# The last up group of quarter 0 as seven products of half blocks, in both feed-forwards

## The reference

```
    h = _rms_norm(x, norm_ffn_pre[i])                                      # first block
    f = jnp.square(jax.nn.relu(h @ w_ffn_up[i])) @ w_ffn_down[i]
    x = x + _rms_norm(f, norm_ffn_post[i])
...
    h = rms_norm(x, norm_mlp[l])                                           # second block
    x = x + jnp.square(jax.nn.relu(h @ w_up[l])) @ w_down[l]
```

## Time and profile before

| what | value |
|---|---|
| median of 3 runs | 1240.69 us (1240.66 to 1241.28) |
| profiled execution, its own time | 1239.91 us |
| its span | 1238.2 us, mean granted TensorE clock 0.997 |
| PE busy | 1205.6 us (97%) |
| DVE busy | 871.9 us (70%) |
| ACT busy | 664.1 us (54%) |
| POOL busy | 420.7 us (34%) |

### The profile page before, as it was taken

One profiled execution on the slowest core, in us unless ns is written; L12 is line 12 of the kernel. 1 busy time (PEld: TensorE's weight loads), 2 busy tenths in 40 slices (PEclk: granted clock), 3 DMA queues, 4 the chain that ended last, 5 costly groups with the idle time before them and its releaser, 6 DMA issues.

```text
span 1238.2 us, 26863 instructions
## 1 busy us (share of the span) xinstructions
PE 1205.6 (97%) x11189; PEld 1103.8 (89%) x11189; DVE 871.9 (70%) x1153; ACT 664.1 (54%) x1154; POOL 420.7 (34%) x345
## 2 busy tenths in 40 slices
PE   8999999998999999999999999999999999999998
PEld 6777797787898999999999997866889999999997
DVE  6678646566468689887895666435576897888953
ACT  4555536557355447456475544544454474564652
POOL 7022226333005247267261141000052472672500
PEclk9999999999999999999999999999999999999999
DMA  6223300002343233333344232122232333333331
GB/s 203 69 68 102 102 2 2 4 3 81 131 150 121 69 103 104 102 103 113 92 171 154 77 107 82 35 69 86 69 101 70 103 103 103 103 107 99 103 120 69
DMA packets 103231, 113.10 MB, mean 91 GB/s; under 512 B 2099, under 2 KB 97381, under 8 KB 103110
## 3 DMA queue, kind: packets, MB, share of 16 engines
q1 hardware_dynamic: 103030, 111.12, 28.4%
q0 software_dynamic: 80, 0.26, 0.1%
HBM read 107.18 MB, written 4.19 MB: 90 GB/s over the span
## 4 chain that ended last, share of the span: by engine, by line
PE 84%; DVE 7%; ACT 4%; issue 2%; DVEq 1%; ACTq 1%; POOL 1%; POOLq 0%
PE ps L627 8%; PE ps L628 7%; PE ps L629 7%; PE ps L718 5%; PE ps L719 5%; PE ps L720 5%; PE ps L591 4%; PE ps L593 4%; PE ps L592 4%; PE ps L773 3%; PE ps L775 3%; PE ps L774 3%; PE ps L678 1%; PE ps L680 1%; PE ps L679 1%
## 5 line engine op out<-in xcount | busy, mean ns | idle before, releaser
L627 PE MATMUL ps<-w_hi,a_hi 128*128 128x256 f32 x640 | 179.5, 280 | 0.3
L628 PE MATMUL ps<-w_lo,a_hi 128*128 128x256 f32 x640 | 178.8, 279 | 0.0
L629 PE MATMUL ps<-w_hi,a_lo 128*128 128x256 f32 x640 | 178.5, 279 | 0.0
L2065 DVE TENSOR_TENSOR w_lo<-w_raw,w_hi 128x2048 fp32r<-128x2048 f32 (+1 forms) x43 | 98.1, 2282 | 45.5 <-ACT w_hi L1398 45.2
L627 PEld LDWEIGHTS ps<-w_hi,a_hi 128*128 128x128 f32 x640 | 120.2, 188 | 1.2 <-DVE w_lo L2194 1.1
L628 PEld LDWEIGHTS ps<-w_lo,a_hi 128*128 128x128 f32 x640 | 120.3, 188 | 0.1
L629 PEld LDWEIGHTS ps<-w_hi,a_lo 128*128 128x128 f32 x640 | 120.3, 188 | 0.0
L718 PE MATMUL ps<-th,w_hi 128*128 128x256 f32 x384 | 109.2, 284 | 1.6 <-ACT tmp L1496 1.6
L720 PE MATMUL ps<-th,w_lo 128*128 128x256 f32 x384 | 107.9, 281 | 0.0
L719 PE MATMUL ps<-tl,w_hi 128*128 128x256 f32 x384 | 107.8, 281 | 0.0
L2173 DVE TENSOR_TENSOR w_lo<-w_raw,w_hi 128x1024 fp32r<-128x1024 f32 (+1 forms) x72 | 100.0, 1403 | 4.4 <-ACT w_hi L1471 4.4
(11 more groups left out here) (467 smaller groups left out, 3885.2 us busy)
## 6 DMA issues: line engine op xcount, KB each, us to landing
w_raw<-w_ffn_up_dram SPq DMA_DIRECT2D x16, 1024.0 KB, 5.7
w_raw<-w_ffn_down_dram SPq DMA_DIRECT2D x16, 1024.0 KB, 5.3
w_raw<-w_up_dram SPq DMA_DIRECT2D x16, 1024.0 KB, 5.8
w_raw<-w_down_dram SPq DMA_DIRECT2D x16, 1024.0 KB, 5.2
w_raw<-w_in_first_dram SPq DMA_DIRECT2D x12, 1024.0 KB, 5.4
w_raw<-w_out_dram SPq DMA_DIRECT2D x8, 1024.0 KB, 5.2
xn<-x_dram SPq DMA_DIRECT2D x8, 512.0 KB, 6.0
w_raw<-w_in_dram SPq DMA_DIRECT2D x4, 1024.0 KB, 6.3
```

The lines of the kernel that those rows point to most:

```text
L627: mm(o, hi[:, hb + k, tok], whi, start=first and own and k == ks[0], stop=False, skip_group_check=True)
L628: mm(o, hi[:, hb + k, tok], wlo, start=False, stop=False, skip_group_check=True)
L629: m = mm(o, lo[:, hb + k, tok], whi, start=False, stop=last and k == ks[-1], skip_group_check=True)
L2065: v.tensor_tensor(w_lo[:, g % 2, :, 0:n], w_raw[:, g % 2, :, 0:n], w_hi[:, g % 2, :, 0:n].bitcast(F32), ALU.subtract).then_inc(sm["w_lo_re ...
```

## The change

In both feed-forwards group 3 of quarter 0 becomes seven products. `seven(0)` is now `range(3, 4)`. Its blocks need room in both slots of `w_hi` and `w_lo`: `A11` and `A12` take the place of channels 0 to 511 of group 2, `SUM2` and `SUM1` that of channels 512 to 1023 of group 2, and `SUM3`, `SUM4` and `A22` lie in the slot that groups 1 and 3 share. So group 2 is now run in halves of the channels (`third_group`): both tiles with channels 0 to 511, a signal (`third_half`), then both tiles with channels 512 to 1023. It has the same 48 matmuls of 512 columns.

POOL makes the four sums of group 3 directly after its activation sums, ahead of the sums of squares. ACT does the four `upper_t` in one go and then the six upper parts of group 3, and only then the square of the second tile of group 1; the two tiles of group 2 are evacuated while group 3 runs. DVE does all four `lower_t` and then six lower parts in the order `A11, SUM3, SUM4, A22, SUM2, SUM1`. The rest of the order is that of a last up group of the other quarters: the first plain down group is split in two halves (`down_upper`, `down_lower`), and results are copied and added in pieces. On SP the load of the second down group now also waits for the sums and the lower part of `A22` of group 3.

```diff
         def seven(q):
-            return range(4 if q else 0)
+            return range(4) if q else range(3, 4)
...
         def block_free(b, q, u, n):
             g = group(b, q, u)
+            if q == 0:
+                return done(g - 1 if n in (SUM3, SUM4, A22) else g)
...
# SP
+                        if q == 0 and c == 1:
+                            sp.wait_ge(sm["wb_lo"], block_at(b, 0, 3, A22))
+                        if c + 2 in seven(q) and c < 2:
                             sp.wait_ge(sm["s_sum"], 4 * seventh(b, q, c + 2) + 4)
...
# TensorE
+            def third_group(b):
+                g, tile = group(b, 0, 2), tile_at(b, 0, 2)
+                for half in range(2):
+                    if half:
+                        pe.wait_ge(sm["w_lo_ready"], g + 1)
+                    else:
+                        pe.wait_ge(sm["third_lo"], b + 1)
+                    for j in range(2):
+                        if half == 0:
+                            pe.wait_ge(sm["tile_evacuated"], tile + j - 3)
+                        o = ps[:, (tile + j) % 4, :]
+                        for k in range(KH * half, KH * (half + 1)):
+                            whi, wlo = (w[:, g % 2, k, j * P:(j + 1) * P] for w in (w_hi, w_lo))
+                            mm(o, whi, h_hi[:, k, :], start=k == 0, stop=False)
+                            mm(o, whi, h_lo[:, k, :], start=False, stop=False)
+                            m = mm(o, wlo, h_hi[:, k, :], start=False, stop=k == KT - 1)
...
# ScalarE, ffn
+                upper_t(b, 2)
+                upper_t(b, 3)
+                upper_a(b, 0, 3)
+                upper_sum(b, 0, 3, SUM3)
+                upper_sum(b, 0, 3, SUM4)
+                upper_a22(b, 0, 3)
+                upper_sum(b, 0, 3, SUM2)
+                upper_sum(b, 0, 3, SUM1)
+                square_high(b, 0, 1, 1)
...
# VectorE, ffn (behind square_low(b, 0, 0, 0) and the two halves of group 2)
+                for j in range(2):
+                    lower_t(b, j)
+                    square_low(b, 0, j, 1 - j)
+                lower_t(b, 2)
+                lower_t(b, 3)
+                for n in (A11, SUM3, SUM4, A22, SUM2, SUM1):
+                    lower_block(b, 0, 3, n)
+                square_low(b, 0, 1, 1)
...
# GpSimd, ffn (behind the three activation sums)
+                sums_s(b, 0, 3)
+                last_sum(b, 0, 3)
                 for u in range(4):
                     sums_dt(b, 0, u)
```

More of the change, by code:

```diff
@@ L356, in block_at @@
         def block_at(b, q, u, n):
-            order = (A11, SUM2, SUM1, A22, SUM4) if u == 0 else (A22, A11, SUM2, SUM1, SUM4)
+            order = (A11, SUM2, SUM1, A22, SUM4) if u == 0 else (A22, A11, SUM2, SUM1, SUM4) if q else (A11, SUM4, A22, SUM2, SUM1)
             return 5 * seventh(b, q, u) + order.index(n) + 1
@@ L723, in seven_products @@
                 pe.wait_ge(sm["tile_evacuated"], tile - 3)
+                if q == 0:
+                    pe.wait_ge(sm["t_sum"], 3 * b + 3)
                 pe.wait_ge(sm["wb_lo"], block_at(b, q, u, A11))
@@ L796, in seven_down @@
                 one(A22, 0, False)
+            def third_group(b):
[14 more added lines that the diff above has]
+                            m = mm(o, wlo, h_hi[:, k, :], start=False, stop=k == KT - 1)
+                        if half:
+                            m.then_inc(sm["mm_done"], 1)
+                        elif j:
+                            m.then_inc(sm["third_half"], 1)
             def ffn(b, n, after_norm):
@@ L802, in ffn @@
                         first_tiles(n, group(b, 0, 0), tile_at(b, 0, 0))
[L803 to L806, removed]
+                        third_group(b)
                     for u in seven(q):
@@ L1468, in block_upper @@
             def block_upper(b, q, u, n, src, count=1):
-                act.wait_ge(sm["mm_done"], block_free(b, q, u, n + count - 1))
+                if q == 0 and n == A11:
+                    act.wait_ge(sm["third_half"], b + 1)
+                else:
+                    act.wait_ge(sm["mm_done"], block_free(b, q, u, n + count - 1))
                 return af(blocks(block_hi, u, n, count), src, ACT.Copy)
@@ L1567, in up @@
                     upper_sum(b, q, u, SUM3)
-                else:
+                elif q:
                     rest(b, q, u - 1)
@@ L1573, in up @@
                 if u == 3:
-                    positive(b, q, 2, 0)
-                    positive(b, q, 2, 1)
+                    if q:
+                        positive(b, q, 2, 0)
+                        positive(b, q, 2, 1)
+                    else:
+                        first_up(b, 2, 0)
+                        first_up(b, 2, 1)
                     down_upper(group(b, q, 4), 0)
                     copied(b, q, u, 1)
+                    if q == 0:
+                        act.wait_ge(sm["t_lo"], 4 * b + 4)
                     square_high(b, q, 2, 0)
@@ L1602, in ffn @@
             def ffn(b):
[L1604 to L1622, removed]
+                for j in range(2):
+                    first_up(b, 0, j)
+                square_high(b, 0, 0, 0)
+                g = group(b, 0, 2)
+                act.wait_ge(w_in[g % 2], landed(g))
+                act.wait_ge(sm["mm_done"], done(g - 1))
+                for half in range(2):
+                    k = slice(KH * half, KH * (half + 1))
+                    m = af(w_hi[:, g % 2, k, :], w_raw[:, g % 2, k, :], ACT.Copy)
+                    m.then_inc(sm["w_hi_ready" if half else "third_hi"], 1)
+                for j in range(2):
+                    first_up(b, 1, j)
+                    upper_t(b, j)
+                    square_high(b, 0, j, 1 - j)
+                upper_t(b, 2)
[7 more added lines that the diff above has]
+                square_high(b, 0, 1, 1)
                 for q in range(4):
@@ L1625, in ffn @@
                         up(b, q, u)
[L1626 to L1630, removed]
+                    rest(b, q, 3)
+                    positive(b, q, 3, 0)
+                    positive(b, q, 3, 1)
+                    square_high(b, q, 3, 0)
                     square_high(b, q, 3, 1)
@@ L2349, in ffn @@
                 sums_t()
-                for u in range(4):
-                    if u == 1:
-                        g = group(b, 0, 2)
-                        dve.wait_ge(sm["third_hi"], b + 1)
[L2354 to L2365, removed]
+                square_low(b, 0, 0, 0)
+                g = group(b, 0, 2)
+                for half in range(2):
+                    if half:
+                        dve.wait_ge(sm["w_hi_ready"], g + 1)
+                        dve.wait_ge(sm["w_lo_ready"], g)
+                    else:
+                        dve.wait_ge(sm["third_hi"], b + 1)
+                    k = slice(KH * half, KH * (half + 1))
+                    m = v.tensor_tensor(w_lo[:, g % 2, k, :], w_raw[:, g % 2, k, :], w_hi[:, g % 2, k, :].bitcast(F32), ALU.subtract)
+                    m.then_inc(sm["w_lo_ready" if half else "third_lo"], 1)
+                for j in range(2):
+                    lower_t(b, j)
[5 more added lines that the diff above has]
+                square_low(b, 0, 1, 1)
                 for q in range(4):
@@ L2368, in ffn @@
                         up(b, q, u)
-                    if q:
-                        square_low(b, q, 3, 0)
+                    square_low(b, q, 3, 0)
                     square_low(b, q, 3, 1)
@@ L3065, in before @@
             def before(b, q, u):
-                if u:
-                    return b, q, u - 1
-                return (b, q - 1, 3) if q > 1 else (b - 1, 3, 3)
+                if q == 0:
+                    return b - 1, 3, 3
+                return (b, q, u - 1) if u else (b, q - 1, 3)
             def sums_dt(b, q, u):
```

9 lines of the change are left out of this document (4 added, 5 removed).

## The result

The changed kernel takes 1250.51 us (median of 4 runs, 1249.98 to 1251.24), the kernel before 1240.99 in the runs beside them: a ratio of 1.0080, 95% interval 1.0068 to 1.0092. It is 9.5 us slower; the forecast was 1249.2 us, in a range of 1242.0 to 1252.5. The profiled execution took 1250.28 us with a span of 1248.6 us.

The account below looks back on a forecast made before the run. PE, busy 97% of the span, was taken as the bound. Per feed-forward -1.25 + 3.23 + 1.80 + 0.48 = +4.26 us, +8.5 in both, gave 1249.2 us on the runs' scale, range 1242 to 1252.5.

Parts of the forecast that it names:

- The saving: PE, group 3 of quarter 0: seven products in place of plain matmuls save 1.25 us in each feed-forward.
- The first stall: PE ahead of A11 in group 3: waits 3.23 us for DVE's lower part, as DVE takes turns with POOL's adds.
- The second stall: PE ahead of SUM2 in group 3: waits 1.80 us for DVE's block subtractions beside POOL's second sums of squares.
- The hitches: End of group 3, from SUM4's last matmul to the down group: 0.48 us over plain matmul time, as in quarter 1.
- The sum: Saving, two stalls and hitches together: +4.26 us in each feed-forward, +8.5 us in both.
- rival 2: Both stalls, and PE's clock falls where it costs, once or twice: 1250.3 to 1252.5 us, chance 0.20.
- The clock: PE's clock may fall after the stalls, costing up to 1.7 us, nothing where the second stall covers it.
- Rivals 3 and 4: 3: POOL delays DVE less, 1241 to 1247 us, chance 0.14; 4: lower parts in time, 1239.2 us, chance 0.13.
- what is hidden: Sums of squares end about 4 us later, at no cost, as PE's down groups shift by the same amount.

Follow-up runs that it names:

- thin sums: The changed kernel, but POOL's four adds of group 3 take 16 elements of a partition in place of 512: 1239.97 us, ratio 0.9994.
- the second set held: The changed kernel, but POOL's second set of sums of squares waits until group 3's last block has its lower part: 1249.11 us, ratio 1.0069.
- The last experiment: Changed kernel with S1 ahead of the second activation sum, DVE reordered, POOL's second squares set held until group 2's first square is lowered: 1242.42 us.

## Why the prediction was right

**The saving.** Forecast 1.25 us a feed-forward. No run shows it by itself, as the joints of the group cost something each time; thin sums give 0.51 us with joints of 0.76, so 1.27 without them. The best stretch was 0.73 us shorter.

**The first stall.** Forecast 3.23 us, from eight DVE subtractions of 7.98 us and eight POOL turns of 6.64 us. Measured 3.21 us, as a wait; as steps it is 3.61 - 0.23 = 3.38 us from the last matmul of group 2. The forecast counts in steps, so 3.38 is the number to set beside 3.23: 0.15 us more. That it is POOL's turns is shown by taking them away in two ways: the four large ones (no stall) and the four small ones (1.05 us left).

**The second stall.** Forecast 1.80 us, measured a wait of 1.40 and a step of 1.56 us too long. The term was 0.24 us too large. PE starts `SUM2` 407.22 - 402.75 = 4.47 us behind `A11`, in place of 4.64, as the blocks are lowered a little faster (starts at 403.66, 404.80 and 405.95). And PE needs `SUM2` 2.91 us behind `A11` in place of 2.84, as its first step behind the first stall is 0.19 us in place of 0.12. The two are 0.17 + 0.07 = 0.24 us. That this stall too is POOL's turns is shown by the second set held, where DVE has `SUM2` in time.

**The hitches.** Forecast 0.48 us, taken from quarter 1. By the same measure, from the last matmul of `SUM4` (412.88 us) to the first of the down group (414.89), it is 2.01 us in place of 1.54: 0.47 us.

**The sum.** Forecast +4.26 us for a stretch, measured +4.31 in the first feed-forward. That it is so near is in part luck: the second stall was 0.24 us smaller than its term, the first in steps 0.15 us larger, and PE's first step behind each of the two, 0.19 and 0.22 us in place of 0.12, added 0.17 us that the sum puts at nothing. In the second feed-forward it was +5.23, of which 0.9 us are the clock. The two make 9.5 us, as much as the medians differ. The spans of the two profiled executions differ by 10.4 us: the other 0.9 us are -0.2 ahead of the first stretch, +0.5 between the two and +0.6 behind the second, with no cause traced. The median, 1250.51 us, is just above the forecast's own range (1247 to 1250.3) and inside that of rival 2; the forecast of 1249.2 is short by about what the clock cost.

**The clock.** Rival 2 had a chance of 0.20, and the traces of the changed kernel bear it out in part: a fall in the second feed-forward in both, in the first in neither; it cost 0.9 us in one trace and nothing in the other. Its cover by the second stall was forecast and is shown by the second set held, where the cover was gone and the fall cost 1.2 us. The chance looks too low; the price, up to 1.7 us by the forecast, was 0.9, 1.2 and 1.4 us where it showed. Only one of the four executions behind the median has a trace: the other three of the changed kernel had mean clocks of 0.992 to 0.996, against 0.997 in the traced one, so they may have lost more. A stall of 3.2 us went with a fall in four of six cases: both feed-forwards with the second set held, the second one in each trace of the changed kernel. By the Trainium skill (TensorE: Matmul & The Clock Gate, What's actually happening) idleness throttles the clock. The traces agree in those four cases and not in the other two.

**Rivals 3 and 4** fell: a POOL add of 512 elements costs DVE about 1.1 us wherever DVE subtracts two SBUF operands at the time. The Trainium skill (GPSIMD Engine Reference, 1. Specifications) names this sharing. The trace agrees: 2.24 us for a subtraction that takes 1.13 alone.

What I argued too lightly is **what is hidden**. That the sums of squares may end 4 us later at no cost held in the changed kernel, as PE is as late itself. The last experiment shows that this cover is thin: once PE was in time, they cost 1.1 us in the down products of each feed-forward.

## What to carry to other kernels

Fewer matmuls are a gain only where the engines that feed them have time left in that very stretch, not on average. Count an engine's queue up to the instruction that PE waits for, and add to it GpSimd's adds that run beside its subtractions of two SBUF operands, here 1.1 us for one of 512 elements and 0.55 for one of 256: VectorE at 70% over the span was at 100% here. And when a reordering removes a wait, look for it at the next place where the moved work is used, and behind that.

## What was not expected of the hardware

The clock of PE fell at a stall of 2.3 us in otherwise full work, in one feed-forward of two, and not at every stall of 3.2 us. Also the first three of POOL's adds of 16 elements lasted 1.00 to 1.20 us beside DVE's subtractions, nearly as long as that subtraction takes alone, while the DVE instruction behind them, 1024 elements at 389.87 us, lasted only 1.24 us: a short POOL add waits for its turn but hardly costs one.
